# A hybrid decoder step on one Trainium2 core: a reordered front, with the S5 drive and readout matmuls split into four of 32 weight columns each

## What is computed

```
proj = rms_norm(x) @ w_in          # q | k | v | u (u: 32 groups x 16 inputs)
attn = window_attend(q, k, v)      # window 128, ALiBi, sinks; samples use a cache
bu   = einsum('gph,blgh->blgp', b_bar, u)            # "drive", complex
xs   = scan(x_t = lam_bar * x_{t-1} + bu_t)          # 32 groups x 64 complex states
y    = einsum('ghp,blgp->blgh', c, xs).real + d * u  # "readout"
y    = gelu(y); y = y * sigmoid(y @ w_glu + b_glu)
h    = x + concat(rms_norm(attn), rms_norm(y)) @ w_out
h   += moe(rms_norm(h))            # top 4 of 32 experts, d_ff 1024
h   += sigmoid(rms_norm(h) @ w_gate) * (p @ w_proj); out = rms_norm(h)
```

## Time and profile before

| | us |
|---|---|
| median of 3 runs | 1353.73 (1352.58 to 1356.2) |
| the profiled execution | 1353.54 |
| its span, first to last instruction | 1351.8 |
| start of the `w_out` matmuls (L832) | 181.5 |
| start of the first expert's up matmuls (L943) | 251.4 |
| PE busy | 1245.0 (92% of the span) |
| mean granted TensorE clock | 0.952 |

### The profile page before, as it was taken

One profiled execution on the slowest core, in us unless ns is written; L12 is line 12 of the kernel. 1 busy time (PEld: TensorE's weight loads), 2 busy tenths in 40 slices (PEclk: granted clock), 3 DMA queues, 4 the chain that ended last, 5 costly groups with the idle time before them and its releaser, 6 DMA issues.

```text
span 1351.8 us, 15552 instructions
## 1 busy us (share of the span) xinstructions
PE 1245.0 (92%) x5966; PEld 612.6 (45%) x5966; DVE 327.2 (24%) x553; ACT 209.9 (16%) x426; POOL 55.1 (4%) x70
## 2 busy tenths in 40 slices
PE   4599678999999999999999999999999999999875
PEld 3497566433434343434434343434344343434354
DVE  7942314112221111121221111111221111111132
ACT  3404712001010110101010110101110101100022
POOL 6600000000000000000000000000000000000000
PEclk9869879989999999999999999999999999998878
DMA  8006413497999999999999999999999999999300
GB/s 262 1 32 239 165 65 125 170 400 319 421 402 417 413 407 424 406 423 406 422 393 421 409 402 423 385 424 410 422 402 422 388 408 415 407 381 359 152 1 33
DMA packets 72238, 438.47 MB, mean 324 GB/s; under 512 B 13616, under 2 KB 16816, under 8 KB 21472
## 3 DMA queue, kind: packets, MB, share of 16 engines
q1 hardware_dynamic: 71632, 437.62, 79.6%
q10 hardware_dynamic: 576, 0.45, 0.1%
HBM read 436.67 MB, written 2.41 MB: 325 GB/s over the span
## 4 chain that ended last, share of the span: by engine, by line
PE 89%; DVE 5%; issue 2%; ACT 2%; DMA 0%; ACTq 0%; DVEq 0%
PE ps L943 38%; PE ps L960 18%; PE ps L929 10%; PE ps L899 5%; PE ps L832 2%; PE ps L1072 2%; PE ps L951 2%; PE ps L902 1%; PE ps L533 1%; PE ps L628 1%; PE ps L577 1%; PE ps L568 1%; PE ps L764 1%; PE ps L1015 1%; PE ps L969 1%
## 5 line engine op out<-in xcount | busy, mean ns | idle before, releaser
L943 PE MATMUL ps<-ring_up,region 128*64 128x512 f32 x2112 | 463.5, 597 | 2.6 <-issue 1.4
L943 PEld LDWEIGHTS ps<-ring_up,region 128*64 128x64 f32 x2112 | 164.1, 138 | 284.0 <-issue 282.1
L960 PE MATMUL ps<-ring_dn,region 128*64 128x512 f32 x1056 | 247.4, 623 | 12.4 <-issue 11.0
L1803 DVE TENSOR_SCALAR region<-ps 128x512 f32<-128x512 f32 x33 | 22.8, 691 | 715.1 <-PE ps L943 715.1
L960 PEld LDWEIGHTS ps<-ring_dn,region 128*64 128x64 f32 x1056 | 82.9, 143 | 163.6 <-issue 161.6
L929 PE MATMUL ps<-region,n_tok 128*128 128x128 f32 (+1 forms) x768 | 136.1, 307 | 0.0
L929 PEld LDWEIGHTS ps<-region,n_tok 128*128 128x128 f32 (+1 forms) x768 | 104.2, 187 | 41.2 <-issue 12.2
L1323 ACT ACTIVATE region<-region 128x512 f32<-128x512 f32 x33 | 20.8, 629 | 501.3 <-DVE region L1803 501.3
L1335 ACT ACTIVATE region<-ps 64x512 f32<-64x512 f32 x66 | 39.1, 592 | 270.4 <-PE ps L960 270.0
L899 PE MATMUL ps<-region 128*128 128x512 f32 (+1 forms) x136 | 68.7, 629 | 2.6 <-issue 1.3
L943 PE MATMUL ps<-region 128*64 128x512 f32 x264 | 62.7, 592 | 0.0
(11 more groups left out here) (359 smaller groups left out, 824.0 us busy)
## 6 DMA issues: line engine op xcount, KB each, us to landing
ring_up<-in_w_up_dram SPq DMA_DIRECT2D x264, 1024.0 KB, 11.9
ring_dn<-in_w_down_dram SPq DMA_DIRECT2D x132, 1024.0 KB, 7.8
ring_up<-in_w_in_dram SPq DMA_DIRECT2D x4, 1280.0 KB, 9.9
ring_dn<-in_w_out_dram SPq DMA_DIRECT2D x1, 4096.0 KB, 20.9
ring_up<-in_w_ple_gate_dram SPq DMA_DIRECT2D x4, 1024.0 KB, 6.7
x_tok<-in_x_prompt_dram SPq DMA_DIRECT2D x2, 512.0 KB
ring_up<-in_w_glu_dram SPq DMA_DIRECT2D x1, 1024.0 KB, 5.1
region<-in_w_ple_proj_dram SPq DMA_DIRECT2D x1, 1024.0 KB
```

The source lines that it names most:

```text
L943: m = mm(ps[64 * (q % 2):64 * (q % 2) + 64, q // 2, :], xe[:, k, slots] if k < UP else one_hot, w, start=(k == 0), stop=(k == UP))
L960: m = mm(ps[64 * half:64 * half + 64, O_B, :], act_t[:, f % 4, 64 * (f // 4):64 * (f // 4) + 64], ring_dn[:, f, 512 * half:512 * half + 51 ...
L1803: V.tensor_scalar(g_lim, bank(0), LIMIT, None, ALU.min).then_inc(Z["g_rdy"], 1)
```

## The change

- **Drive and readout.** Each matmul of `drive`, `drive_samples` and `read_out` becomes four, each with 32 of the 128 weight columns and the 32 output partitions that belong to them; the four follow each other for each tile. `drive` goes from 16 to 64 matmuls a half, `drive_samples` from 32 to 128, `read_out` from 48 to 192.
- **PE's order.** The four u projections stand together, behind them all transposes of `e_bd`, then both drives and the samples', `within_blocks`, and only then all six k, v, q projections. The parameter transposes stand behind `project_u(0)`. The second attention block's values stand ahead of the samples' values; both transposes of the attention output stand behind the S5 sums of squares.
- **ACT's order.** The copies to `u_blk` are 16 of 32 x 256 and alternate with the 8 copies to `e_t`; both stand behind the sines. `within_copies` stands ahead of all six copies of `qkv`. Gelu is split: 8 copies on ACT and 8 on DVE move the readout to `y_t`, then one gelu of 128 x 1056. The two attention roots are one.
- **Who does what.** POOL keeps the `f_bd` zeroes and its half of `intra`; DVE takes the other zeroes, the phases and the POOL half of `f_bd`; ACT takes the small copies into `f_bd` and the decay. DVE's norm scaling and the `fa` products are interleaved with the parameter chain.
- **DMA.** `w_in` comes in two column parts, u first. The S5 matrices and the old state move from SP's queue to ACT's, the norm vectors from ACT's to SP's, behind x.

```diff
-            for r, name in enumerate(("ssm_b_re", "ssm_b_im")):
-                sp.dma_start(b_raw[:, r], ...).then_inc(ld_b, 16)
...
-            for k in range(0, KD, 2):
-                sp.dma_start(w_in[:, k:k + 2], w[:, k:k + 2]).then_inc(ld_win, 16)
+            for arrived, cols in ((ld_wu, slice(D_IN - D_SSM, D_IN)), (ld_win, slice(0, D_IN - D_SSM))):
+                for k in range(0, KD, 4):
+                    sp.dma_start(w_in[:, k:k + 4, cols], w[:, k:k + 4, cols]).then_inc(arrived, 16)
...
+            for r, name in enumerate(("ssm_c_re", "ssm_c_im")):
+                act.dma_start(c_raw[:, r], A[name][0].rearrange("(k g) h p -> (g h) k p", k=4)).then_inc(ld_c, 16)
+            for r, name in enumerate(("ssm_b_re", "ssm_b_im")):
+                act.dma_start(b_raw[:, r], A[name][0].rearrange("(k g) p h -> (g p) k h", g=2)).then_inc(ld_b, 16)
...
             def drive(half):
...
                 for r in range(2):
                     for i in range(8):
-                        m = mm(ps[:, (6, 0)[half] + r, BLOCKS * i:BLOCKS * (i + 1)], e_t[:, r, 8 * half + i],
-                               u_blk[:, 8 * half + i], start=True, stop=True)
+                        for p in range(0, P, 32):
+                            m = mm(ps[p:p + 32, (6, 0)[half] + r, BLOCKS * i:BLOCKS * (i + 1)],
+                                   e_t[:, r, 8 * half + i, p:p + 32], u_blk[:, 8 * half + i], start=True, stop=True)
...
             def read_out(half):
...
-                    out = ps[:, 2 + half, BLOCKS * (i % 8):BLOCKS * (i % 8 + 1)]
+                    out = [ps[32 * t:32 * t + 32, 2 + half, BLOCKS * (i % 8):BLOCKS * (i % 8 + 1)] for t in range(STEPS)]
                     for r in range(2):
-                        mm(out, f_bd[r][:, i, 1:].rearrange("p j g h -> p (j g h)"), states[:, r, i, 0:BLOCKS],
-                           start=(r == 0), stop=False)
-                    m = mm(out, intra[:, i], u_blk[:, i], start=False, stop=True)
+                        for t in range(STEPS):
+                            mm(out[t], f_bd[r][:, i, 1 + t].rearrange("p g h -> p (g h)"), states[:, r, i, 0:BLOCKS],
+                               start=(r == 0), stop=False)
+                    for t in range(STEPS):
+                        m = mm(out[t], intra[:, i, 32 * t:32 * t + 32], u_blk[:, i], start=False, stop=True)
...
+            def unit_input():
+                act.wait_ge(Z["y_rot"], 2)
+                for t in range(2):
+                    for q in range(4):
+                        m = f(y_t[32 * q:32 * q + 32, :, t:SEQ:STEPS], by_step[32 * t:32 * t + 32, :, q], ACT.Copy)
+                m.then_inc(Z["ypre"], 1)
+                act.wait_ge(Z["ypre"], 3)
+                f(y_t, y_t, ACT.Gelu_apprx_tanh).then_inc(Z["gelu"], 1)
...
-            qkv((0, 1))
             within_copies()
-            qkv((2, 3, 4, 5))
+            qkv()
```

More of the change, by code:

```diff
@@ L418, in chain @@
                 pool.wait_ge(pool_step, n[0])
-            tt = nc.gpsimd.tensor_tensor
+            for r in range(2):
+                chain(nc.gpsimd.memset(f_bd[r], 0.0))
+            nc.gpsimd.nop().then_inc(Z["zeroed"], 2)
             chain(nc.gpsimd.memset(b_down[NE:2 * NE], 0.0))
             chain(nc.gpsimd.memset(b_down[2 * NE:P], 0.0))
[L424 to L454, removed]
-            pool.wait_ge(Z["s5_sb"], 1)
-            pool.wait_ge(Z["turned_ps"], 2)
-            s1, s2 = (fb_flat[:, 1024 * a:1024 * a + 1024].rearrange("p (i j h) -> p i j h", i=ST, j=STEPS)
-                      for a in range(2))
-            tt(s1, every_step(c_cc[:, 0], STEPS), per_step(0, STEPS), ALU.mult)
@@ L460, in _ @@
-            chain(tt(s2, every_step(c_cc[:, 1], STEPS), per_step(1, STEPS), ALU.mult))
-            for par in range(2):
-                g = slice(par * S, par * S + S)
-                chain(tt(f_bd[0][g, :, 1:, par], s1[g], s2[g], ALU.add))
-            nc.gpsimd.nop().then_inc(Z["f_sb"], 1)
             def lay(k, q):
@@ L1118, in _ @@
                     act.wait_ge(ld_x, 64)
+                    f(stat[:, 0, 3:4], eps, ACT.Sqrt)
                 f(n_tok[0:nt, c], x_tok[0:nt, c], ACT.Square, accum_out=stat[0:nt, c, 0:1]).then_inc(Z["norm_ssq"], 1)
-            roots(0)
+                root(0, c)
+            act.wait_ge(Z["vec_ps"], 1)
+            f(vecs[:], bank(7, V_N), ACT.Copy).then_inc(Z["vec_sb"], 1)
             act.wait_ge(Z["par_red"], 3)
@@ L1159, in drive_copies, with block_copies @@
-            def drive_copies(half):
-                for n_ in range(4 * half, 4 * half + 4):
-                    r, quad = n_ % 4 // 2, 2 * half + n_ % 2
-                    act.wait_ge(Z["e_ps"], n_ + 1)
-                    f(e_t[:, r, 4 * quad:4 * quad + 4], ps[:, 4 + n_ % 2].rearrange("p (k n) -> p k n", k=4), ACT.Copy
-                      ).then_inc(Z["e_sb"], 1)
-            act.wait_ge(Z["phase"], 1)
+            def block_copies(k):
+                for q in range(4):
+                    m = f(u_blk[32 * k:32 * k + 32, q::4], ps[32 * q:32 * q + 32, 0:4, STEPS - 1 - k:SEQ:STEPS], ACT.Copy)
+                return m
@@ L1171, in _ @@
-            drive_copies(0)
-            block_copies(1)
-            drive_copies(1)
+            act.wait_ge(Z["u_ps"], 4)
+            for k in range(STEPS):
+                block_copies(k)
+                drive_copy(2 * k)
+                drive_copy(2 * k + 1)
+            for q in range(4):
+                f(u_s[0:32, q::4], ps[32 * q:32 * q + 32, 0:4, SEQ:T], ACT.Copy)
+            f(proj[:, 6:10, SEQ:T], ps[:, 0:4, SEQ:T], ACT.Copy).then_inc(Z["us_sb"], 1)
             def lay(k, q):
@@ L1393, in halves @@
                 return x.rearrange("k (g p) -> k g p", g=2)
+            for r in range(2):
+                V.memset(e_bd[r], 0.0).then_inc(Z["zeroed"], 1)
+            V.memset(m_flat, 0.0).then_inc(Z["zeroed"], 1)
+            V.memset(decay.rearrange("p (i b) -> p i b", i=ST)[:, :, 0:1], 0.0)
             dve.wait_ge(Z["par_exp"], 1)
@@ L1668, in _ @@
             spread_queries()
+            unit_input()
             attended(0)
```

280 lines of the change are left out of this document (144 added, 136 removed).

## The result

The changed kernel is slower: 1362.49 us median (1360.53 to 1367.15) against 1353.15 for the kernel before, a ratio of 1.0068 with a 95% interval of 1.0045 to 1.009. Forecast were 1345.9, and a range from 1337 to 1354. The profiled execution took 1360.53, its span is 1358.7. A few executions of this study, at 1511 to 1560 us at a lower granted clock and one of e11 at 3144 us, are left out of all ratios.

The account below looks back on a forecast made before the run. The front up to `w_out` (181.5 us) was taken to decide the result, loop and tail moving as a block. Savings of 3.7 to `kv_to_tokens` and 3.9 to `w_out` gave 1353.5 - 7.6 = 1345.9 us, range 1337 to 1354.

Parts of the forecast that it names:

- What bounds the kernel: Whole kernel: expert loop and tail move as a block with the start of `w_out`, 181.5 us; the front decides the result.
- Start: Kernel start to first `e_bd`: first Exp at 11.6 us instead of 7.17, `e_bd` at 42.2, 0.7 earlier.
- 4.7 for the hold, five more issues of 0.4: ACT's load issues at the start: 4.7 us held at the second b load, then five issues; free at 10.3.
- ACT held: Rival at the start: b loads sharing DMA with `w_in` hold ACT longer, 1358.3 us if first Exp at 24; chance 0.08.
- To the first drive: From `e_bd` to the first drive: phases 3.9, sines 2.1, copies 12.0 us; drive at 60.2, first half done 64.7.
- To the last projection: First drive to `kv_to_tokens`: DVE's chain, then third projection waiting on ACT until 93.0; `kv_to_tokens` at 110.1 instead of 113.8.
- The readout: Readout split into 384 records of 17 ns: 6.5 us instead of 10.7, bounds 4.3 and 11.7.
- the rival's 30.5: Rival on the split matmuls: a 32-column record costs 30.5 ns, readout gains nothing, 1354.5 us; chance 0.11.
- A cold readout: Rival in the readout: PE's clock drops during it, readout takes 13.0 us, total 1352.4; chance 0.11.
- To `w_out`: From `kv_to_tokens` to `w_out`: gated unit starts 30.8 us in, `w_out` at 63.8 instead of 67.7, so at 173.9.
- The sum: Whole kernel: 3.7 + 3.9 = 7.6 us saved, 1353.5 - 7.6 = 1345.9, some +-5.

Follow-up runs that it names:

- e11: Changed kernel with ScalarE's copies of the states and cache transposes ahead of its readout copies and gelu; ratio 0.9989 to the kernel before.
- e14: Changed kernel with SyncE waiting for the b loads to land before it issues the w_in loads; ratio 1.001 to the kernel before.
- e1: Changed kernel with the two state loads moved from ScalarE's queue to SyncE's, ahead of w_in; 1351.6 us median, ratio 0.9995 to the kernel before.

## Why the prediction was wrong

**What bounds the kernel: right.** The front up to `w_out` is what the change moves. That the rest moves as a block holds to +-4 us only; here it was 4.3 us shorter, which hid part of the loss and was luck.

**Start: wrong, the term "4.7 for the hold, five more issues of 0.4".** I priced the state loads at an ordinary issue each. The first took 9.73 and the second 1.04; the hold at the second b load was 5.53. All the rest of this step holds when shifted: from the Exp to `e_bd` I counted 30.6 and it was 29.3, DVE's 4.58 did go.

This was my rival *ACT held*. I gave it 0.08 and argued against it with SP's hold, which was over at 7.75. That row had x ahead of the b loads and `w_in` behind them in one queue; it says nothing about `w_in` beside them. I had the rule at hand too and drew the wrong end from it: the Trainium skill ("DMA: Bandwidth & Descriptors", "Queues, rings and completion order") says that an engine takes whole packets in turn. The trace agrees, with 1032 packets of the one queue beside 1031 of the other. In turn by the packet is a poor share for a queue of small packets: 64 bytes of b for 2 or 3 KB of `w_in` each time. The 24.2 us of the changed kernel and the 8.4 of e14 bear out the rule and not my reading of it. My price for the rival, one us of result per us of hold, was right: in e1 the Exp ran 10.6 us earlier, and 9.9 were gained.

**To the first drive: right.** From `e_bd` to the drive I counted 18.0, it was 17.5, with phases 3.9, sines 2.0 and copies of 0.38 each (0.40 taken). The first half took 3.38 instead of 4.4, at a mean clock of 0.57 where I had 0.50.

**To the last projection: right.** VectorE's chain was 9.8 a half as counted, and the new wait, ACT's copies into `intra`, ended a gap of 8.47 us (about 6 forecast). The third projection came 7.3 after my 93.0; 7.0 of that stood already at the end of the first half of the drive, 71.7 for my 64.7.

**The readout: the record's price right, the step wrong.** A record takes 14 ns at 1.00 (120 of them from 120.60 to 122.30), under my 17 and far from the rival's 30.5; I was right there. But the step 384 x 17 ns = 6.5 took the engine's rate for the rate at which it can go on; with instructions for 128 records per 6.2 us it took 13.9. None of my rivals had that. *A cold readout* ended near the size (13.0) with another cause. A price from a short row was drawn out over a long one: the 64 records at 11.3 ns (`read_out_samples`, the second line of the earlier trace rows; the first line is `within_blocks`) are half a packet's worth and showed no gap. The rule that I set aside there, that matmuls never start under about 25 ns apart (the Trainium skill, "TensorE: Matmul & The Clock Gate", "Wait — 56ns, not 53.3ns?"), doesn't hold between neighbours here, 14 ns; as a mean over a long quiet run it comes out near, 3.35/128 = 26 ns, by the supply of instructions. By that rule my sum would have been 1349.0, not the 1348 that I wrote: 9.6 for the readout is 3.1 more than 6.5.

**To `w_out`: 3.9 too low in all.** Between readout and gated unit I counted 21.3 and it was 26.4: 1.5 is a third gap of the supply (137.06), 0.9 the eight readout copies at 0.61 instead of 0.5, 2.1 the cold stretch, 12.9 for my 10.8, and some 0.5 the copies of the probabilities. Before, the same work ran at 1.00 in 8.07. I had seen that the idle time would chill it, and sized it by half. From there to `w_out` 24.6 after the gated unit, 25.7 counted: right.

**The sum.** 7.6 late at `kv_to_tokens`, 7.3 in the readout and 3.9 behind it are the 18.8 us by which `w_out` came after the forecast; the 4.3 by which the rest was shorter in this profile leave 14.5 of the 14.6 between 1345.9 and 1360.53.

## What to carry to other kernels

Splitting an instruction into pieces that each take less time only pays as long as the instruction supply keeps up: set the number of new instructions against what is fetched in that stretch, above all where large loads fill the DMA engines, and try the coarser split first. Before loads are moved to a compute engine's queue, ask what is queued beside them on the other queue, and put nothing behind loads of many small packets. Where an engine copies for two consumers, let it serve first the one that stands still.

## What the runs showed of the hardware that I had not expected

TensorE's instructions arrive 256 at a time (128 matmul records with their weight loads), one packet of 16 KB each. Where PE ran out, it resumed 3.3 to 4.0 us apart with the DMA engines quiet and 5.8 to 6.9 apart while slabs were loading, always 1.2 to 1.5 us after a packet's end. In these kernels the 384 short records used up 128 faster than that and stopped; 192 at the same place ran on what was in store. A stop can go with a lower clock: after the one of 4.36 us it was at 0.50, after the one of 1.82 still at 1.00.

A readout record cost 111 ns with 128 weight columns, 31 with 64 and 14 with 32, all at clock 1.00 with 64 moving columns. For the same 128 columns that makes 111, 62 and 56: nearly all that there was to gain lay in the first halving.

The second of two b loads of 128 KB (64 bytes a packet) landed in 8.4 us with `w_in` held back and in 24.2 beside 5 MB of `w_in` on the other queue; there the next load of the same queue held its engine for 9.73 us.
